# Five small edits to a hybrid encoder layer on one core: order of early copies, order of small matmuls, a narrower low-rank product, an activation moved into a loop, and a split last gating

## The reference

```python
h = rms_norm(x, norm1_g)
proj = h @ w_in
gq, gk, gv, gog, glr_f, glr_b, dq, dk, dv = jnp.split(proj, offs, axis=-1)
a = gla_mixer(...)        # z_f = (glr_f @ wg_f) + bg_f; chunks of 64; forward and backward; out * silu(gog)
d = diff_attention(...)   # 4 heads, two softmax maps a head, QK-norm and rotary
x = x + concat(a, d) @ w_out
x = x + expert_choice_ffn(rms_norm(x, norm2_g))   # 16 experts, each takes its top rows, SwiGLU of width 2048
```

## Time and profile before

| | |
|---|---|
| median of 3 runs | 1631.16 us (lowest 1629.38, highest 3914.66) |
| the profiled execution | 1630.23 us, of which 1628.4 us from first to last instruction |
| mean granted TensorE clock | 0.972 of full speed |
| PE busy | 1526.7 us (94%) |
| DVE busy | 1258.4 us (77%) |
| ACT busy | 1053.9 us (65%) |
| POOL busy | 130.1 us (8%) |
| chain that ended last | PE 83%, DVE 7%, issue 5%, ACT 2%, DMA 1% |

### The profile page before, as it was taken

One profiled execution on the slowest core, in us unless ns is written; L12 is line 12 of the kernel. 1 busy time (PEld: TensorE's weight loads), 2 busy tenths in 40 slices (PEclk: granted clock), 3 DMA queues, 4 the chain that ended last, 5 costly groups with the idle time before them and its releaser, 6 DMA issues.

```text
span 1628.4 us, 18264 instructions
## 1 busy us (share of the span) xinstructions
PE 1526.7 (94%) x7244; PEld 1113.2 (68%) x7244; DVE 1258.4 (77%) x1137; ACT 1053.9 (65%) x1070; POOL 130.1 (8%) x95
## 2 busy tenths in 40 slices
PE   5999999766994999999999999999999999999996
PEld 4787777445882777777777777777777777777774
DVE  5259586487437889888898888988889888888884
ACT  6434232575213777777777787777877878778774
POOL 1023122000000010100000000000000101000000
PEclk9999999898996999999999999999999999999999
DMA  6111011300138999999999999999999999999991
GB/s 235 53 52 52 1 53 53 142 1 3 78 119 292 374 365 379 374 394 373 378 387 360 395 369 388 376 367 395 374 384 374 377 384 365 392 380 376 381 368 56
DMA packets 192004, 448.58 MB, mean 275 GB/s; under 512 B 12688, under 2 KB 13232, under 8 KB 191920
## 3 DMA queue, kind: packets, MB, share of 16 engines
q1 hardware_dynamic: 187440, 433.16, 71.8%
q0 software_dynamic: 3904, 12.62, 3.4%
q10 hardware_dynamic: 576, 1.64, 0.3%
HBM read 434.80 MB, written 12.58 MB: 275 GB/s over the span
## 4 chain that ended last, share of the span: by engine, by line
PE 83%; DVE 7%; issue 5%; ACT 2%; DMA 1%; POOL 0%; POOLq 0%; SPq 0%; DVEq 0%; ACTq 0%
PE ps L781 21%; PE ps L779 21%; PE ps L780 21%; PE ps L518 5%; PE ps L519 5%; PE ps L520 5%; PE ps L812 1%; DVE st L1397 1%; PE ps L718 1%; DVE states L1243 1%; DMA slice_raw<-in_w_in 1%; PE ps L706 1%; PE ps L772 1%; DVE t L1258 1%; PE ps L698 1%
## 5 line engine op out<-in xcount | busy, mean ns | idle before, releaser
L1543 DVE TENSOR_TENSOR wl<-raw,wh 128x2048 fp32r<-128x2048 f32 x384 | 875.1, 2292 | 142.2 <-ACT wh L1103 137.0
L1103 ACT CAST wh<-raw 128x2048 fp32r<-128x2048 f32 x384 | 730.7, 1912 | 133.7 <-PE ps L781 132.6
L779 PE MATMUL ps<-wh,XTh 128*96 128x512 f32 x1024 | 407.3, 398 | 1.2 <-DVE XTl L1548 1.2
L781 PE MATMUL ps<-wl,XTh 128*96 128x512 f32 x1024 | 405.1, 396 | 0.0
L780 PE MATMUL ps<-wh,XTl 128*96 128x512 f32 x1024 | 402.2, 393 | 0.0
L781 PEld LDWEIGHTS ps<-wl,XTh 128*96 128x96 f32 x1024 | 165.0, 161 | 72.3
L780 PEld LDWEIGHTS ps<-wh,XTl 128*96 128x96 f32 x1024 | 166.0, 162 | 68.6
L779 PEld LDWEIGHTS ps<-wh,XTh 128*96 128x96 f32 x1024 | 165.5, 162 | 68.2 <-DVE XTl L1548 1.5
L779 PE MATMUL ps<-wh,gTh 128*96 128x512 f32 x512 | 201.9, 394 | 1.2 <-DVE gTl L1554 1.2
L781 PE MATMUL ps<-wl,gTh 128*96 128x512 f32 x512 | 201.1, 393 | 0.0
L780 PE MATMUL ps<-wh,gTl 128*96 128x512 f32 x512 | 200.7, 392 | 0.0
(11 more groups left out here) (220 smaller groups left out, 1446.5 us busy)
## 6 DMA issues: line engine op xcount, KB each, us to landing
raw<-in_w_gate SPq DMA_DIRECT2D x128, 1024.0 KB, 8.7
raw<-in_w_up SPq DMA_DIRECT2D x128, 1024.0 KB, 8.8
raw<-in_w_down SPq DMA_DIRECT2D x128, 1024.0 KB, 9.1
slice_raw<-in_w_in SPq DMA_DIRECT2D x6, 2048.0 KB, 9.2
X<-in_x_sample SPq DMA_DIRECT2D x8, 512.0 KB, 10.4
slice_raw<-in_w_out SPq DMA_DIRECT2D x2, 2048.0 KB, 10.6
X<-in_x_prompt SPq DMA_DIRECT2D x4, 512.0 KB, 4.9
h_rows<-hn SPq DMA_DIRECT2D x4, 512.0 KB, 2.7
```

Of the source, the lines that this page charges most:

```text
L779: pe.matmul(out, hi, rhs_h, start=first, stop=False)
L781: return pe.matmul(out, hi, rhs_l, start=False, stop=last)
L1103: act.copy(wh[:, n % CONV, :], raw[:, n % RAW, :]).then_inc(s_wh, 1)
L1543: dve.tensor_tensor(wl[:, n % CONV, :], raw[:, n % RAW, :], wh[:, n % CONV, :].bitcast(F32), ALU.subtract).then_inc(s_wl, 1)
```

## The change

It has five parts.

1. ACT's stream has `norm_turned(0)` and `norm_turned(1)` ahead of `high_parts(0)`.
2. The low-rank units hold the high and the low weights side by side in one tile `wlr2` of 64 columns. One matmul of 64 output rows makes high x high (PSUM rows 0 to 31) and low x high (rows 32 to 63); one of 32 output rows adds high x low. `lrT` and `wg` become 64 rows, with the gate weights held twice (two more small transfers on POOL's queue), so that the gate matmul adds the two parts.
3. In `scores` and `updates` the loop over row tiles is outside and the loop over halves inside.
4. Silu is applied to the first five units of OG inside the last slice; the sixth goes from PSUM through Silu straight to OG (`gate_unit`).
5. In the last tile of the last expert the first 512 columns are finished ahead of the second; ACT gates them while PE works on, and of the second 512 columns ACT takes the prompt rows and DVE the sample rows. POOL waits for both.

```diff
@@ scores, updates
-                for d in range(2):
-                    for t in range(n):
+                for t in range(n):
+                    for d in range(2):
...
-                for odd in range(2):
-                    r = slice(odd * CHUNK, (odd + 1) * CHUNK)
-                    for t in range(n):
+                for t in range(n):
+                    for odd in range(2):
+                        r = slice(odd * CHUNK, (odd + 1) * CHUNK)
@@ unit "lr"
+                    both = ps[0:4 * RANK, b, 0:n * P].rearrange("p (t c) -> p t c", t=n)
                     for k in range(KD):
-                        mm = three(ps[0:2 * RANK, b, 0:n * P].rearrange("p (t c) -> p t c", t=n),
-                                   wlrh[:, k, :], wlrl[:, k, :],
...
+                        if k >= 1:
+                            pe.matmul(both[0:2 * RANK], wlrh[:, k, :], HTl[:, t0:t0 + n, k, :], start=False, stop=False)
+                        mm = pe.matmul(both, wlr2[:, k, :], HTh[:, k, t0 * P:(t0 + n) * P]
+                                       .rearrange("p (t c) -> p t c", t=n), start=(k == 0), stop=(k == KD - 1))
+                        if k == 0:
+                            pe.matmul(both[0:2 * RANK], wlrh[:, k, :], HTl[:, t0:t0 + n, k, :], start=False, stop=False)
@@ POOL, gate weights
+            for r in (0, 2 * RANK):
+                pool.dma_start(wg[r:r + RANK, :, 0:DK], a["gla_wg_f"][0].rearrange("r (h d) -> r h d", h=HEADS))\
+                    .then_inc(s_wg, 16)
+                pool.dma_start(wg[r + RANK:r + 2 * RANK, :, DK:P],
+                               a["gla_wg_b"][0].rearrange("r (h d) -> r h d", h=HEADS)).then_inc(s_wg, 16)
@@ ACT, behind the first two roots
-            high_parts(0)
             norm_turned(0)
             norm_turned(1)
+            high_parts(0)
@@ ACT, last slice
+            def gate_unit():
+                u = len(UNITS) - 1
+                act.wait_ge(s_unit, u + 1)
+                act.activation(OG[:, NT - 1, :], ps[:, u % 4, :], ACT.Silu).then_inc(s_free_a, 1)
...
+                    else:
+                        act.wait_ge(s_free_a, n_free_a - 1)
+                        act.activation(OG[:, 0:NT - 1, :], OG[:, 0:NT - 1, :], ACT.Silu).then_inc(s_ego, 1)
-            act.wait_ge(s_free_a, n_free_a)
-            act.activation(OG[:], OG[:], ACT.Silu).then_inc(s_ego, 1)
@@ PE, last tile of the last expert
+                    final = n == NTI - 1
+                    for f, half in ((0, 0), (1, 0), (0, 1), (1, 1)) if final else ((0, 0), (0, 1), (1, 0), (1, 1)):
...
+                        if final and (f, half) == (1, 0):
+                            mm.then_inc(s_ylast, 1)
@@ ACT, end
-            gated(NE - 1)
+            e = NE - 1
+            act.wait_ge(s_ylast, 1)
+            act.wait_ge(s_add, 32 * (e - 1))
+            act.mul(Ys[e % 2][0:CAP_S, 0:512], ps[0:CAP_S, 4, :], gate[0:CAP_S, e:e + 1])
+            act.mul(Yp[e % 2][0:CAP_P, 0:512], ps[CAP_S:CAP, 4, :], gate[CAP_S:CAP, e:e + 1]).then_inc(s_y, 1)
+            act.wait_ge(*tile_used("d", NQ - 1))
+            act.mul(Yp[e % 2][0:CAP_P, 512:D], ps[CAP_S:CAP, 5, :], gate[CAP_S:CAP, e:e + 1]).then_inc(s_y, 1)
@@ DVE, end
+            e = NE - 1
+            dve.wait_ge(*tile_used("d", NQ - 1))
+            dve.wait_ge(s_add, 32 * (e - 1))
+            dve.tensor_scalar(Ys[e % 2][0:CAP_S, 512:D], ps[0:CAP_S, 5, :], gate[0:CAP_S, e:e + 1], None, ALU.mult)\
+                .then_inc(s_ylast, 1)
```

More of the change, by code:

```diff
@@ L145, in build @@
         wlr = at("wlr", 49152, [P, KD, 2 * RANK])
-        wlrh = at("wlrh", 50176, [P, KD, 2 * RANK], F32R)
-        wlrl = at("wlrl", 51200, [P, KD, 2 * RANK], F32R)
+        wlr2 = at("wlr2", 50176, [P, KD, 4 * RANK], F32R)
+        wlrh, wlrl = wlr2[:, :, 0:2 * RANK], wlr2[:, :, 2 * RANK:4 * RANK]
         junk1 = at("junk1", 53248, [P, D])
@@ L189, in build @@
         gcol = at("gcol", 211328, [P, KD])
-        wg = at("wg", 212992, [2 * RANK, HEADS, P])
-        lrT = at("lrT", 215040, [2 * RANK, TOK])
+        wg = at("wg", 212992, [4 * RANK, HEADS, P])
+        lrT = at("lrT", 215040, [4 * RANK, TOK])
         aff = at("aff", 215040, [96, 2 * P])
@@ L475, in add_rows @@
                 pool.wait_ge(s_y, 2 * (e + 1))
+                if e == NE - 1:
+                    pool.wait_ge(s_ylast, 2)
                 if e >= 1:
@@ L797, in use_tile @@
                     s = q % NS
-                    for f in range(2):
+                    final = n == NTI - 1
+                    for f, half in ((0, 0), (1, 0), (0, 1), (1, 1)) if final else ((0, 0), (0, 1), (1, 0), (1, 1)):
                         ff = 2 * part_ + f
-                        for half in range(2):
-                            d = slice(half * 512, (half + 1) * 512)
-                            mm = products(ps[0:CAP, 4 + half, :], (gTh[:, ff, :], gTl[:, ff, :]),
-                                          h_[:, f, d], l_[:, f, d], s == 0 and ff == 0,
-                                          s == NS - 1 and ff == FC - 1)
+                        d = slice(half * 512, (half + 1) * 512)
+                        mm = products(ps[0:CAP, 4 + half, :], (gTh[:, ff, :], gTl[:, ff, :]),
+                                      h_[:, f, d], l_[:, f, d], s == 0 and ff == 0,
+                                      s == NS - 1 and ff == FC - 1)
+                        if final and (f, half) == (1, 0):
+                            mm.then_inc(s_ylast, 1)
                 mm.then_inc(s_used, 1)
@@ L893, in copy_unit @@
                     t0, n = (0, T_PROMPT) if t == 0 else (T_PROMPT, T_SAMPLE)
-                    last = act.copy(lrT[:, t0:t0 + n], ps[0:2 * RANK, b, 0:n])
+                    last = act.copy(lrT[:, t0:t0 + n], ps[0:4 * RANK, b, 0:n])
                 elif kind == "rope":
@@ L970, in _ @@
             act.wait_ge(s_wlr, 16)
-            act.copy(wlrh[:], wlr[:]).then_inc(s_lrh, 1)
+            act.copy(wlrh, wlr[:]).then_inc(s_lrh, 1)
             for c in range(4):
@@ L999, in _ @@
                         act.wait_ge(s_qt, 2 * HEADS)
-                    copy_unit("tok", FIRST + h, t)
+                    if i == BODY - 1:
+                        gate_unit()
+                    else:
+                        copy_unit("tok", FIRST + h, t)
                 if t == NT - 1 and h + 1 < HEADS:
@@ L1373, in beside @@
                     dve.wait_ge(s_ego, 1)
+                    dve.wait_ge(s_free_a, n_free_a)
                 if i < 4 * NT:
```

13 lines of the change are left out of this document (4 added, 9 removed).

## The result

| | before | changed |
|---|---|---|
| median | 1630.27 us (4 runs) | 1613.31 us (4 runs; 1612.23 to 1613.96) |
| ratio, with its 95% interval | | 0.9892 (0.9881 to 0.9904) |
| span of the profiled execution | 1628.4 us | 1612.1 us |
| mean granted TensorE clock | 0.972 | 0.973 |

The change takes 17.0 us off, or 16.3 between the two profiled spans; the ratio's interval reaches from 15.7 to 19.4. The forecast was 1614.4. One of the four executions of the kernel before took 3914.66 us, the other three 1628.60 to 1631.16; 48 more, taken beside the later experiments, have medians of 1630.56 to 1631.00. I go through the timeline of the changed kernel in the order of the parts; a row is start, length, engine, line, operation, tiles, shape, count, and the idle time ahead.

What follows compares the result with a forecast made beforehand. PE bounds the untouched expert stage; ACT's order, PE or DVE limit places ahead, ACT the tail. 5.5 + 2.75 + 2.55 + 3.85 + 2.05 = 16.7 us off 1631.16 gives 1614.4; range 1612.5 to 1616.5 (0.58), wider 1610.5 to 1619.5.

Steps and rivals of the forecast that it cites:

- head 1's scores: Scores of head 1 with halves in turn: PE's next matmul at 157.61 instead of 158.56, 0.95 us earlier.
- Part 1: Start of the kernel: ACT copies turned tiles ahead of its casts; 5.5 us less, bounds 2.0 and 5.8.
- the 0.1 that I kept for it: Start: ACT, some 3 us late against PE, was taken to catch up to 0.1 when PE needs the last tile.
- Part 2: Low-rank units: 32 of 48 matmuls remain, 5.5 us instead of 8.25, so 2.75 us less.
- The width rival: Low-rank units: 28 changes of output width are paid, costing 5.0 us more, total 1619.4; chance 0.15.
- the 0.18: Cost in us of one change of output width, worked out from GLA outputs alternating widths 128 and 64.
- the entry to the units: Start of the low-rank units, width 128 to 32: spacing 0.23 us as inside a unit, so a change costs nothing.
- Part 3: Scores and state updates, halves in turn: 0.49 at head 0, 0.95 at head 1, 2 x 0.55 in updates; together 2.55 us.
- Part 4: End of the last slice: Silu moved ahead, so the first exponential comes 3.85 us earlier; bounds 2.3 and 4.1.
- The cover: Last slice: ACT free by 298.6, 0.15 us or more before the last unit at 298.76; each 0.1 over costs 0.1.
- Part 5: Tail: gating split over ACT and DVE lets POOL start three instructions earlier, 2.05 us less; bounds 1.4 and 2.1.
- The rival of the moving clock: 1.2 GHz stretches follow PE's idle times, 3.2 us each: one less gives 1611.2, one more 1617.6; chance 0.12.

Runs made afterwards that it cites:

- a_out: Changed kernel with the GLA outputs grouped by width, 4 changes of width per head instead of 12: 1611.72 us, ratio 0.9879.
- the low-rank pair: Changed kernel with its low-rank units in plain float32, widths alternating or grouped: 1632.47 and 1629.34 us, the units 24.45 and 21.31 us.
- the seven old-order profiles: Profiles with halves outside the tile loop: kernel before (twice), with the first, second, fourth or fifth edit alone, changed kernel without the third; scores 1 to next 2.92 to 3.88 us.
- p5_tail: Kernel before with only the last gating split over ScalarE and VectorE and over two halves of columns: 1629.38 us, ratio 0.9990.
- the fourteen profiles: All profiles on record, of the kernel before, the changed kernel and their variants: seven with the old order of halves, seven with the new; attention 87.48 to 90.08 us.
- p3_halves: Kernel before with only the row halves alternating in scores and updates, gate matmuls still on 32 rows: 1627.49 us, ratio 0.9974.
- a_no3: Changed kernel with row halves outside the loop over tiles again, in scores and updates: 1617.64 us, ratio 0.9916.

## Why the prediction was right

1614.4 was forecast and 1613.31 measured. All steps but two, head 1's scores and the tail, hold by their own marks; that the sum comes out so near is partly luck, as shown below.

- **Part 1**, 5.5: 5.7 to 5.8 from the first transpose on (the table's second row). ACT caught up fully: the 0.1 that I kept for it and its 1.0 us later casts cost nothing. The first transpose moved by 0.35 for a reason outside the change.
- **Part 2**, 2.75: 2.69, and 0.19 more in head 1's block, the only block with a gate where PE is the limit. The width rival is out for this type: the 0.18 that I worked out from the earlier trace rows was near the truth for plain float32 (0.17 by `a_out`, 0.13 by the low-rank pair), and it was right to trust the entry to the units for the reduced type. Why the types differ no run shows.
- **Part 3**, scores: head 0 0.49, heads 2 and 3 nothing, as worked out. Head 1's 0.95 was measured (3.87 to 2.92) and still wrong as a step: "156.78 + 0.68 + 0.15 = 157.61 instead of 158.56" took the low clock of one profile for a property of the kernel. At full clock the old order gives 2.92 too, and the new one gains nothing. Under the low clock the order does count: the changed kernel's scores lay partly under it (2.22 us), and PE still waited for DVE. So the step is worth 0 to 0.95 by the execution (0.49 on the mean of the seven old-order profiles), and should have stood in the sum as that range.
- **Part 3**, updates: 0.55 a head, and only where PE is the limit, holds; heads 0 and 2 show it as idle time (46.9 us to the next scores in all kernels).
- **Part 4**, 3.85: 3.85. The cover that the prediction put at 0.15 or more comes to 0.1 when its own figures are added (293.32 + 3 x 0.59 + 1.28 + 2.3 = 298.67 against 298.76); measured, ACT waits 0.43 for the last unit.
- **Part 5**, 2.05: 1.45. "POOL starts three instructions earlier" left out what the split adds: a third wait (0.46), and DVE's slightly longer scaling and signal (0.06, and 0.13 that is near the scatter).

At equal clock the steps give 5.8 + 2.7 + 0.5 (head 0) + 0.8 (head 1's block: 0.55 + 0.19, seen as 44.03 to 43.25, which is 41.85 + 1.4) + 0.5 (head 3's) + 3.85 + 1.45 = 15.6 us. Against that my sum of 16.7 has 0.95 too much at head 1 and 0.6 in the tail, and 0.3 too little in part 1 and 0.2 in the blocks. The medians say 17.0. The 1.5 us by which the low stretches cost less with the new order, on the mean of the fourteen profiles, make it 17.1: 0.4 of them lie between scores 1 and scores 2, and 1.1 from scores 3 on, where my sum had nothing but the updates. So two steps were too large, what happens behind head 3 was missing, and the errors nearly cancelled: that 16.7 lies so near is partly luck.

The rival of the moving clock, to which I gave 0.12, had hold of the mechanism that mattered. Its sentence "The stretches follow PE's idle times" holds only in part: ahead of head 1's scores PE stands idle for 2.85 us in the kernel before and in `p5_tail` alike, and the clock is low behind it in the one and full in the other.

The medians give part 3 3.4 us when it is added to the kernel before and 4.3 when it is taken from the changed one, the fourteen profiles 3.1; with intervals of 1.6 us and more to either side these agree. What stays open is why a low stretch costs less behind head 3 with the new order. Five of seven against none of seven is hardly chance, but the kernels of the fourteen profiles differ in other things too; only `p3_halves` and `a_no3` differ from a neighbour by the order alone, with one profile each.

## What to carry to other kernels

Work out what an edit is worth at either level of the clock before crediting it: a stretch at half clock in one profile may be a matter of that execution, and a second profile of the same kernel shows which stretches move. Group matmuls of equal width where operands are plain float32; in the reduced type, widths of 64 and 32 alternated here at no cost. When a last step is split over two engines, let both count on one semaphore. When one profile of each kernel leaves a difference open, compare the same stretch over all profiles that share its code.

## What the hardware showed that I had not expected

- A change of output width between 64 and 32 costs 0.13 us in plain float32 (24.45 and 21.31 us with 28 and 4 changes) and nothing in the reduced float32 type with the same tiles (5.56 us with 28). Between 128 and 64 in plain float32 it is up to 0.17 (4.73 and 3.35 us with 8 changes fewer).
- Plain float32 matmuls on 64 rows of the array that follow a gate on 64 rows instead of 32 save 0.19 us (3.89 to 3.70); with the halves in turn as well, the two kinds overlap.
- One more wait ahead of GpSimd's gather-and-add delays it by 0.46 us after the last signal (0.85 and 0.40 us behind DVE's end).
- Attention with the same code takes 87.5 to 90.1 us; between 87.7 and 90.1, 2.3 us come from one 1.2 GHz stretch that lasts 7 us instead of 3.5.
